# Accumulating each expert block's rows in DRAM instead of storing them per expert and adding them on chip

## The reference

```python
h = rmsnorm(x, norm_ffn_g[i])
x = x + hierarchical_moe(h, ...)
# in hierarchical_moe, per block of up to 128 tokens of one expert:
hid = jax.nn.silu(xb @ w_gate[e]) * (xb @ w_up[e])
yb = hid @ w_down[e]
# and at its end, over the two experts of each token:
out = jax.ops.segment_sum(y_sorted * w_sorted[:, None], tok, num_segments=n_tok)
```

## Time and profile before

| | |
|---|---|
| median of 3 runs | 2259.09 us (2257.99 to 2264.34) |
| profiled execution | span 2255.5 us, from the first to the last instruction; its time beside the span is not given |
| TensorE busy | 2009.1 us, 89% |
| VectorE busy | 1592.5 us, 71% |
| ScalarE busy | 1365.6 us, 61% |
| GpSimd busy | 336.2 us, 15% |
| mean granted TensorE clock | 0.951 of full speed |
| DMA | 553.90 MB; the queue of SyncE 61.6% and that of GpSimd 5.3% of the engines' span |

### The profile page before, as it was taken

The page is one execution under the profiler, slowest core; times in us unless marked ns, Lnnn a source line. Parts: engine busy times, 40 slices in busy tenths (PEclk is TensorE's granted clock), DMA queues, the critical chain, the costliest instruction groups (busy, mean ns, idle before and its releaser), DMA issues.

```text
span 2255.5 us, 32390 instructions
## 1 busy us (share of the span) xinstructions
PE 2009.1 (89%) x9356; PEld 1662.5 (74%) x9356; DVE 1592.5 (71%) x1887; ACT 1365.6 (61%) x1746; POOL 336.2 (15%) x338
## 2 busy tenths in 40 slices
PE   7999999999829999999999579896499999999980
PEld 5887878887717888888887468675388888878870
DVE  3335343443558999999998676747599999889875
ACT  3442233522417888888888533434288888888872
POOL 1000000000031111212211230001311121122214
PEclk9999999999959999999999879998699999999995
DMA  7231223322536999999999642116489999999966
GB/s 266 94 97 62 94 94 101 94 75 85 192 122 226 378 381 382 379 388 372 380 380 366 243 173 93 57 65 252 127 295 374 382 377 380 379 365 381 386 255 231
DMA packets 165993, 553.90 MB, mean 246 GB/s; under 512 B 31525, under 2 KB 33733, under 8 KB 163760
## 3 DMA queue, kind: packets, MB, share of 16 engines
q1 hardware_dynamic: 139728, 511.99, 61.6%
q0 software_dynamic: 26208, 41.19, 5.3%
HBM read 540.57 MB, written 47.78 MB: 261 GB/s over the span
## 4 chain that ended last, share of the span: by engine, by line
PE 39%; DMA 33%; issue 11%; DVE 9%; POOLq 3%; POOL 3%; ACT 1%; DVEq 0%; SPq 0%; ACTq 0%
DMA y_rows<-big,metas 19%; PE bank L486 13%; PE bank L487 12%; PE bank L488 12%; DMA metas<-lists 12%; POOLq L426 2%; DVE big L981 2%; POOL lists L416 1%; POOL big L437 1%; DVE a_lo L970 1%; DVE bank L1071 1%; PE bank L500 1%; DVE x_res L996 1%; DMA big<-normed,metas 1%; DMA big<-y_rows 1%
## 5 line engine op out<-in xcount | busy, mean ns | idle before, releaser
L486 PE MATMUL bank<-w_hi,a_hi 128*128 128x512 f32 x1816 | 727.5, 401 | 26.2 <-DVE a_lo L970 15.9
L488 PE MATMUL bank<-w_hi,a_lo 128*128 128x512 f32 x1816 | 713.4, 393 | 0.0
L487 PE MATMUL bank<-w_lo,a_hi 128*128 128x512 f32 x1816 | 712.5, 392 | 0.0
L970 DVE TENSOR_TENSOR w_lo<-raw,w_hi 128x1024 fp32r<-128x1024 f32 x384 | 456.9, 1221 | 349.6 <-ACT w_hi L716 348.3
L716 ACT ACTIVATE w_hi<-raw 128x1024 fp32r<-128x1024 f32 x384 | 405.8, 1061 | 465.9 <-PE bank L488 458.2
L970 DVE TENSOR_TENSOR w_lo<-big,w_hi 128x1024 fp32r<-128x1024 f32 x522 | 612.6, 1221 | 45.8 <-ACT w_hi L716 30.1
L716 ACT ACTIVATE w_hi<-big 128x1024 fp32r<-128x1024 f32 x522 | 536.5, 1064 | 72.4 <-PE bank L488 62.8
L486 PEld LDWEIGHTS bank<-w_hi,a_hi 128*128 128x128 f32 x1816 | 345.1, 190 | 104.0 <-issue 22.6
L488 PEld LDWEIGHTS bank<-w_hi,a_lo 128*128 128x128 f32 x1816 | 343.8, 189 | 74.2
L487 PEld LDWEIGHTS bank<-w_lo,a_hi 128*128 128x128 f32 x1816 | 344.6, 190 | 67.3
L970 DVE TENSOR_TENSOR a_lo<-bank,a_hi 128x512 fp32r<-128x512 f32 x263 | 170.1, 684 | 106.6 <-ACT a_hi L716 106.6
(11 more groups left out here) (140 smaller groups left out, 1646.9 us busy)
## 6 DMA issues: line engine op xcount, KB each, us to landing
big<-in_w_down SPq DMA_DIRECT2D x260, 512.0 KB, 7.2
big<-in_w_up SPq DMA_DIRECT2D x254, 512.0 KB, 6.8
raw<-in_w_gate SPq DMA_DIRECT2D x252, 512.0 KB
raw<-in_a_w_in SPq DMA_DIRECT2D x64, 512.0 KB, 4.0
raw<-in_a_w_out SPq DMA_DIRECT2D x32, 512.0 KB, 3.2
big<-y_rows SPq DMA_DIRECT2D x16, 1024.0 KB, 6.5
normed<-big SPq DMA_DIRECT2D x4, 2048.0 KB, 9.3
raw<-in_b_w_in SPq DMA_DIRECT2D x16, 512.0 KB, 3.5
```

Source lines behind the costliest of these rows:

```text
L486: pe.matmul(dst, left_hi, right_hi, start=first, stop=False)
L487: pe.matmul(dst, left_hi, right_lo, start=False, stop=False)
L488: return pe.matmul(dst, left_lo, right_hi, start=False, stop=last)
L970: return nc.vector.tensor_tensor(dst, src, f32(hi), ALU.subtract)
```

## The change

The output rows are no longer stored per choice. In each layer the residual is stored to a DRAM tensor `x_sum` (SyncE, after each half's normalized rows), and each block's scatter adds its rows to it: a DMA with `compute_op=ALU.add`, addressed by the token's index, word 0 of the list entry. The bounds test of the scatter is gone. So that unfilled list rows have a place to go, the lists are filled with zeros (weight 0) and an index of 1024 + row within the block, and `x_sum` has 128 spare rows, which are filled from the input at the start; the gather still leaves them out, as they lie beyond its bound of 1023. At the end of the stage SyncE loads each tile of `x_sum` (512 KB) straight into `x_res`, all eight at once; the buffers `comb`, GpSimd's addition and VectorE's `add` are gone, and ScalarE's squares wait for the tile's load. GpSimd waits for the stores of `x_sum` before its loop.

```diff
-        y_rows = [dram(f"y_rows{n}", (2 * SEQ, D), F32) for n in range(LAYERS)]
+        x_sum = [dram(f"x_sum{n}", (SEQ + P, D), F32) for n in range(LAYERS)]
...
                     sp.dma_start(normed[L].rearrange("(t p) d -> p t d", p=P)[:, h * HT:(h + 1) * HT, :],
                                  hn[h]).then_inc(M.stored[h], 16)
+                    x_final(h)
+                    sp.dma_start(x_sum[L][0:SEQ, :].rearrange("(t p) d -> p t d", p=P)[:, h * HT:(h + 1) * HT, :],
+                                 x_res[:, h * HT:(h + 1) * HT, :]).then_inc(M.x_stored, 16)
...
-                yv = y_rows[L].rearrange("(t p k) d -> p t k d", p=P, k=2)
                 for t in range(TT):
-                    if t >= COMBS:
-                        sp.wait_ge(M.added, t - COMBS + 1)
-                    sp.dma_start(comb[t % COMBS], yv[:, t, :, :]).then_inc(g.comb[t % COMBS], 16)
+                    sp.dma_start(x_res[:, t, :], x_sum[L][t * P:(t + 1) * P, :]).then_inc(g.x_back[t], 16)
...
-            pool.memset(bu[:, 0:1024], 1.0).then_inc(g.init, 1)
+            pool.memset(bu[:, 0:1024], 0.0).then_inc(g.init, 1)
             pool.wait_ge(g.init, 2)
+            spare = bu[:, 0:1024].bitcast(I32).rearrange("p (b r w) -> p b r w", r=BLK, w=4)
+            pool.iota(spare[:, :, :, 0:1].rearrange("p b r w -> p b (r w)"), [[0, 2], [1, BLK]], SEQ, 0).then_inc(g.init, 1)
+            pool.wait_ge(g.init, 3)
             for L in range(LAYERS):
+                pool.dma_start(x_sum[L][SEQ:SEQ + P, :], A["x"][0, 0:P, :]).then_inc(g.lists_ready, 16)
...
                     pool.indirect_dma_start(
-                        out=y_rows[L][:, :],
-                        out_offset=bass.IndirectOffsetOnAxis(ap=meta_s[:, 1:2], axis=0),
+                        out=x_sum[L][:, :],
+                        out_offset=bass.IndirectOffsetOnAxis(ap=meta_s[:, 0:1], axis=0),
                         in_=y_sb.rearrange("p n f -> p (n f)"), in_offset=None,
-                        bounds_check=2 * SEQ - 1, oob_is_err=False).then_inc(M.scattered, 16)
+                        compute_op=ALU.add).then_inc(M.scattered, 16)
...
                 pool.wait_ge(M.table, 1)
+                pool.wait_ge(M.x_stored, 16 * HALVES)
...
-                for t in range(TT):
-                    pool.wait_ge(g.comb[t % COMBS], 16 * ((L * TT + t) // COMBS + 1))
-                    two = comb[t % COMBS]
-                    pool.tensor_tensor(two[:, 0, :], two[:, 0, :], two[:, 1, :], ALU.add).then_inc(M.summed, 1)
...
             def norm_added(L, n, h, base, t):
-                act.wait_ge(m[L].added, base + t + 1)
+                act.wait_ge(g.x_back[base + t], 16 * (L + 1))
...
-            add_and_norm(1, 8, (0, 1), TT)
+            for h in range(HALVES):
+                norm(8 + h, h, h * HT)
```

More of the change, by code:

```diff
@@ L38 @@
 ROUND = GU + DN
-COMBS = 4
 BLK = P
@@ L121, in encoder_trunk @@
         hid = bv[:, 6144 + F:6144 + 2 * F]
-        comb = [bu[:, n * 2048:(n + 1) * 2048].rearrange("p (k d) -> p k d", k=2) for n in range(COMBS)]
         x_hi = a_hi[:, 0:2, :].rearrange("p a (k t) -> p (a k) t", t=P)
@@ L173, in encoder_trunk @@
                        "sq", "var", "std", "rstd", "waited", "hn", "t_full", "t_hi", "t_lo", "out_stored"],
-                 {"x_loaded": HT, "comb": COMBS})
+                 {"x_loaded": HT, "x_back": TT})
         RINGS = ["hi", "lo", "used"]
@@ L185, in encoder_trunk @@
                "h_full", "h_hi", "h_lo", "y_out", "meta_s", "scattered",
-               "added", "small", "summed"]
+               "small", "x_stored"]
         m = [sems(f"moe{n}", MOE, {"raw": ROUND, "stored": HALVES}) for n in range(LAYERS)]
@@ L236, in _, with moe @@
             sgu_half(1, False)
-            def moe(L, before_lo, before_y, next_weights):
+            def moe(L, before_lo, before_y, x_final, next_weights):
                 M = m[L]
@@ L336, in _ @@
             sp.sem_inc(q.lo, RING)
-            moe(0, lambda e: e.wait_ge(s.lo, RING + 2 * SU), lambda e: e.wait_ge(s.y_lo, 2 * 2 * KC), pool_first)
+            moe(0, lambda e: e.wait_ge(s.lo, RING + 2 * SU), lambda e: e.wait_ge(s.y_lo, 2 * 2 * KC),
+                lambda h: sp.wait_ge(s.ev_dve, BANKS + (h + 1) * S_EVD), pool_first)
             for u in range(RING, HALVES * PV):
@@ L359, in _ @@
             moe(1, lambda e: e.wait_ge(q.lo, RING + total), lambda e: e.wait_ge(q.y_lo, HALVES * KC),
-                lambda: None)
+                lambda h: sp.wait_ge(q.ev_dve, (h + 1) * BANKS), lambda: None)
             ov = out.rearrange("o (t p) d -> p (o t) d", p=P)
@@ L409, in moe @@
                 load_gain(2 * L + 2, A["norm_mix_g"][1] if L == 0 else A["final_norm_g"])
-                pool.wait_ge(g.lists_ready, 16 * LAYERS)
+                pool.wait_ge(g.lists_ready, 16 * 2 * LAYERS)
                 for t in range(TT):
@@ L469, in moe @@
                 scatter(n - 1)
-                pool.wait_ge(M.gathered, 16 * (n + 1))
-                waited()
-                for t in range(TT):
-                    pool.wait_ge(g.comb[t % COMBS], 16 * ((L * TT + t) // COMBS + 1))
-                    two = comb[t % COMBS]
-                    pool.tensor_tensor(two[:, 0, :], two[:, 0, :], two[:, 1, :], ALU.add).then_inc(M.summed, 1)
             moe(0)
@@ L791, in _ @@
                         act.wait_ge(g.small, 16 * 8)
-                        act.wait_ge(g.lists_ready, 16 * LAYERS)
+                        act.wait_ge(g.lists_ready, 16 * 2 * LAYERS)
                         u_banks(c4 - 3)
@@ L990, in norm @@
                     normed_tile(n, h, base, t)
[L992 to L1005, removed]
             def transposed(n):
@@ L1317, in _ @@
                 if u == 3:
-                    add_and_norm(0, 4, (1,), HT)
+                    norm(4, 1, 0)
                     transposed(4)
                 t = u - (PV - HT)
-                if t >= 0:
-                    add(0, HT + t)
                 unit(u)
```

## The result

The changed kernel takes 2378.28 us (median of 4 runs, 2374.32 to 2383.09), the kernel before 2261.72 in the same session. The ratio is 1.0505, 95% interval 1.0462 to 1.0548: 5% slower. The prediction was 2383.

What follows compares the result with a forecast made beforehand. GpSimd's serial ring, level with TensorE and the DMA engines, was taken to bound the kernel. Loop scatters + 157, layer ends - 39, last scatters + 6 make + 124, so 2383 us; range 2265 to 2600.

Steps and rivals of the forecast that it cites:

- The bound and the ring: First loop: GpSimd's serial scatter landing, list read and issue take 17.91 us per block, within 1% of TensorE and DMA.
- The price of the accumulation: Each loop scatter: twice the bytes per row adds 2.7 us to landing, 10.3 instead of 7.6.
- Rival 2: Loop scatters: only the destination's read counts, unfilled rows use other engines; + 1.4 us each, 2307 us; chance 0.22.
- Rival 3: Loop scatters: read and write one after the other, + 6.3 us each, 2591 us; granted clock could fall; chance 0.21.
- The rule of two reads: Accumulating scatter: two reads per piece on one ring, about half the rate, so doubled row traffic is about right.
- The volume: Loop block: 7.57 MB at 379 GB/s takes 20.0 us, + 2.1; an estimate not added to the 2.7.
- The loops: Both layers' loops: 58 scatters in GpSimd's ring at 2.7 us more each, + 157 us.
- The ends: Layer ends: direct loads without additions gain 16.7 us in layer 1 and 22.4 in layer 2, together 39.1.
- The last scatters: Last two scatters of each layer, under little load: + 1.5 us each, half a landing, 6 us in all.
- Edits at nothing: x_res stores, covered by VectorE's routing, the iota and small copies in the first mixer stage: no added time.

Runs made afterwards that it cites:

- e4: Changed kernel, with the scatter's index copied aside so GpSimd awaits its landing only before the next scatter: 2272.34 us, 1.0044 of the kernel before.
- e1: Changed kernel, with unfilled list rows left out of the adding scatter: 2371.67 us, 1.0473 of the kernel before.
- e7: Changed kernel, adding scatter of 128 half rows, the other half of each row left out: 2295.42 us, 1.0123 of the kernel before.
- e8: Changed kernel, plain scatter of 128 half rows, no sum: 2222.42 us, 0.9801 of the kernel before.
- e9: Kernel before with GpSimd's landing wait moved later, and accumulating loads replacing loads and both additions at layer ends: 2258.91 us, 0.9943 of before.
- e3: Changed kernel, plain scatter of the filled rows only, sum over experts left out: 2219.35 us, 0.9811 of the kernel before.
- e5: Kernel before, with GpSimd's wait for the scatter's landing moved to ahead of the next scatter: 2248.01 us, 0.9920 of the kernel before.
- e6: Changed kernel, adding only filled rows, with GpSimd's landing wait moved to before the next scatter: 2270.52 us, 1.0028 of the kernel before.

## Why the prediction was right

**The bound and the ring: right.** The forecast rested on GpSimd's ring being closed and level with TensorE. The 58 waits for mere issue are there after as before, the block grew by 20.65 - 17.91 = 2.74 us (by 2.66 over the same window in both kernels) where the landing, counted from the issue, grew by 2.6 and the list read's by 0.1, and opening the ring (e4) took some 105 us away.

**The price of the accumulation: right in size, wrong in part of its reason.** Forecast 2.7 us per scatter, measured 2.6 (10.2 - 7.6), landing 10.2 against 10.3. But it was reckoned as twice the bytes per row at the transport's price. e1 shows that the unfilled rows cost no landing, and e7 with e8 that half or more of the surplus doesn't depend on the bytes. With the 0.8 us that the bytes cost (1.3 by the packets), and no fixed part, that reasoning alone would have given 46 us (75) instead of 157. The bytes were priced too dear and the fixed part was not in the sum at all; that the two make up for each other to 0.1 us is luck. Rival 2 had the rows right (they travel beside) and its price, 1.4, too low for the whole. Rival 3 was right in that there is a part besides the bytes, but of 1.2 to 1.7 us and not a gather of 6.3; its fall of the granted clock did not come either (0.99 in the loop). Its 20 us of idle TensorE are not in the earlier trace rows, which shows 10. The rule of two reads at about half the rate (the Trainium skill, page "Collectives: The Full Stack", section "The bandwidth ceiling: the fold count and why AG ≠ RS ≠ AR", said there of a reduce in a collective) agrees with the engines' time in e9, 2.54 us per load against 1.26, and says nothing of the landing, which decided here.

**The volume: wrong as a bound.** 20.0 us per block was reckoned from 379 GB/s; e4 moves the same in 18.82. It was not the term taken, so it cost nothing here.

**The loops: 156 us where 157 + 3 were forecast.** 58 scatters x 2.6 = 151, and the next-to-last of each layer 2.6 more.

**The ends: right, a little small.** - 40.8 against - 39.1, and - 44.9 with the 4.1 us behind the first end, which the prediction put at nothing as hidden; e3 shows 43 by itself.

**The last scatters: too small.** The surplus at little load was taken as 1.5 us each, half a landing; the last ones land 3.1 later. Like the surplus in the loop it shrinks little with the bytes (2.0 with half rows, e7 and e8).

**Edits at nothing: right in sum.** The stores of x_res take 14.8 us each to land, and the last list scatter of the router 9.03 instead of 3.94 us, but it is issued 3 us earlier (652.63 against 655.73) and the list read behind it takes 1.9 instead of 4.0, so that the first gather goes out at 664.75 against 664.83. Before, then after:

```profile
655.73 3.94 DMA lists<-payload,place
659.95 3.98 DMA metas<-lists
664.83 3.98 DMA big<-normed,metas
```

```profile
652.63 9.03 DMA lists<-payload,place
661.94 1.91 DMA metas<-lists
664.75 3.82 DMA big<-normed,metas
```

**Which version.** The kernel of e5, the old scheme with the ring opened, is faster than both (0.992 of before). The new ends are worth 43 us (e3), but only with a sum that the loop then has to pay for: with the ring open, accumulating (e6) is still 22 us behind e5.

## What to carry to other kernels

Look for the ring that one queue forms with itself before pricing a transfer: where an engine waits for each landing in order, a transfer costs its latency once per turn, whatever engines it leaves free, and the cheap cure is to move the wait behind the work that doesn't need it. An accumulating DMA costs twice over: a fixed part in latency, which fewer rows don't shorten, and the engines' time. Work that sits on some of the DMA engines only is weighed by those, not by the sum of bytes. A rate seen in a trace is what the kernel asked for; only an experiment that asks for more shows what there is.

## What the runs showed of the hardware that was not expected

- An accumulating scatter of 4 KB rows lands 2.5 us after a plain one, with 63 or 128 rows (10.1 and 10.2 against 7.8 and 7.7), and with little load as well (5.8 against 3.3). With rows of 2 KB the surplus is 2.1.
- Its instruction takes at least 1602 ns on GpSimd, the plain one 985.
- Accumulating loads from DRAM into SBUF ran at 205 GB/s with the DMA share at 1.06 and landed 2.54 us apart, plain ones of the same 512 KB 1.26 us. A 4 KB packet takes 327 ns where it adds and 159 where not.
- Where only the first of the 128 rows of a scatter are in bounds, eight of its 16 landing records come early and eight late (e1, e6); with all rows adding they come together (after, e4).
- Taking half of the accumulated rows away freed the weights' transfers hardly at all (18.58 against 18.82 us per block), though the rate fell from 373 to 364 GB/s.
